# Compressed scores of the prompt with the keys stationary, and three of four groups' normalisation and turning inside the attention loop

## The chip, the cores and the metric

The kernel runs on one core of one Trainium2 chip. Its metric is the time of one execution in device microseconds (us). The engines of the core are TensorE (PE; PEld is its weight load), VectorE (DVE), ScalarE (ACT), GpSimd (POOL) and SyncE (SP). Each takes its own instructions in the order in which they are written; they meet only in semaphores.

## What is computed

One inference step of a hybrid decoder layer: 512 prompt tokens and 8 single decode tokens go through one input projection, an attention group of 16 heads in three branches (compressed, selected, window), a state-space group, an output projection and an MLP. The change lies in the compressed branch of the prompt. There the keys are 31 compressed blocks for each of 4 KV groups, and each group serves 4 heads:

```python
def compressed_attention(q, kc, qpos):
    n_cmp = kc.shape[1]
    s = jnp.einsum('btgrd,bngd->bgrtn', q, kc[:, :, 0]) * ATTN_SCALE
    blk_last = jnp.arange(n_cmp) * CMP_STRIDE + (CMP_BLOCK - 1)
    p = masked_softmax(s, blk_last[None, :] <= qpos[:, None])
    o = jnp.einsum('bgrtn,bngd->btgrd', p, kc[:, :, 1])
    return o.astype(q.dtype), p

def gate_branches(gates, o_cmp, o_sel, o_win):
    return gates[..., 0, None] * o_cmp + gates[..., 1, None] * o_sel + gates[..., 2, None] * o_win
```

For 512 tokens the selected branch covers all blocks, so the two other branches are causal attention of 512 queries over 512 keys, with keys and values of their own.

## The kernel before

The program is one long list for each engine, without a scheduler: the order of the functions at its end (L2421 onward) and the order of the lines in them is the order of the work. The stages around the change, with their lines, are these.

- The input projection ends with `proj`, the projected columns of all 520 tokens, transposed. `rows_*` (L735 to L772) turns keys and values back into token order and writes them out.
- `stack_act` and `stack_dve` (L916 to L950) make the operands of the prompt's attention. PE multiplies in a short float format (fp32r), so a query head of 64 rows is stacked over its own rounding rest in one tile of 128 rows: ACT writes the high part (L923, 64x512), DVE the rest (L940). The keys of a branch and group get two tiles, high over high (`k_hh`) and rest over rest (`k_ll`): ACT writes one half of `k_hh` (L930), DVE both halves of `k_ll` (L949, two instructions) and the second half of `k_hh` (L950). The list `STACKED` holds 16 steps: 4 steps with 8 query heads, 4 with keys (groups 0 and 1, both branches), then the same for the other 8 heads and groups 2 and 3. A key tile lies where a projected query column lay; so the table `K_AFTER` makes a key step wait for query steps (`as_lo`).
- `gate_act` (L978 to L981) puts the gates through a sigmoid. `cmp_p_*` (L805 to L850) makes the compressed keys and values: first layer on PE (L813), sum on DVE (L842), SiLU on ACT (L834), second layer on PE (L818, L823), bias on DVE (L847, L850). `kcp_high` and `kcp_low` (L956, L966, L967) split the keys into `kc_hh` and `kc_ll`, 32 columns for each group. `q_dve` (L1416) puts the decode tokens' queries in place.
- `att_cmp_pe/dve/act` (L985 to L1071) is the compressed attention of the prompt. `scores_c(g)` takes, for each of 4 heads and 4 tiles of 128 queries, the queries as weights and streams 32 columns of `kc_hh` and of `kc_ll`: 32 matmuls a group, in bank 4 or 5 of PSUM by turns (`CB`). DVE adds the mask, takes the maximum and subtracts it (`shifted`, L1025 to L1032), ACT takes the exponential (L1064), DVE sums, inverts, multiplies by the gate and scales (`normed`, L1038 to L1048), PE turns the result with 4 transposes into bank 6 (L1012), and ACT copies it to `kv_tok` (L1070), where the values' product later reads it (`pcT`). Groups 2 and 3 take the banks and buffers of groups 0 and 1. All four groups are through before the attention loop turns its first probabilities.
- `att_pe/dve/act` (L1085 to L1195) is the attention loop: 32 units `u`, one for each head (`h = u // 2`) and branch (`b`). In a unit PE does the scores of unit u+1 (`score`, L1081 to L1083, 4 query tiles into banks 0 to 3), the value product of unit u-1 (`values`, L1112, and at odd units the compressed branch, L1117) and ten transposes of the probabilities of unit u (`turn`, L1100, banks 4 to 6). DVE does `factors` (L1162 to L1168), the maxima of unit u+1 (`row_max`, L1156), the finished head at even units (`head_out`, L1174) and two copies of turned probabilities (`turned`, L1182, L1184). ACT does the exponentials of unit u+1 (`exps`, L1138) and one copy (L1148). Unit 0's `score` stands ahead of the loop, in `att_cmp_pe`.

On POOL, `q_pool` (L1263) clears `qz` and `values_pool` (L802) then clears `vbd`. After the loop come the decode tokens' attention, the state-space part, the output projection and the MLP; none of them is touched.

## Time and profile before

| | us |
|---|---|
| median of 3 runs | 2975.57 |
| their range | 2968.17 to 2980.98 |
| profiled execution | 2988.49 |
| its span in the trace | 2986.8 |

| stretch of the trace, us | what runs |
|---|---|
| 704 to 717 | turning of keys and values |
| 717 to 750 | stacking, gates, compressed keys and values |
| 750 to 796 | compressed attention of the prompt, and `score` of unit 0 |
| 796 to 974 | attention loop |

The page of the profile gives the busy time of each engine over the span; the timelines give single instructions with their start, and in brackets how long the engine had been idle and what released it. A row with a count merges instructions of one kind that follow one another. The duration of a matmul holds the time of its way through the array, so the pace of matmuls is read from start to start. PEclk is the granted clock of TensorE, 1.00 for 2.4 GHz and 0.50 for 1.2 GHz.

### The profile page before, as it was taken

How to read it: one execution, taken by the hardware profiler on the slowest of the kernel's cores; microseconds unless marked ns; L12 is line 12 of the kernel's file. 1: busy time of each engine (PE TensorE's matmuls, PEld its weight loads, DVE VectorE, ACT ScalarE, POOL GpSimd, SP SyncE). 2: the span in 40 equal slices, each digit the busy share in tenths (PEclk: the TensorE clock that was granted, in tenths of full speed). 3: DMA queues.
4: the chain of work that ended last, by engine and by line, in shares of the span. 5: the costliest groups of instructions: out<-in, count | busy, mean ns of one | idle time of the engine just before them, and what ended most of it. 6: DMA issues, size and time to landing. Idle time of an engine off the chain costs nothing.

```text
span 2986.8 us, 51003 instructions
## 1 busy us (share of the span) xinstructions
PE 2820.8 (94%) x21260; PEld 2613.5 (88%) x21260; DVE 1122.8 (38%) x1659; ACT 803.9 (27%) x1277; POOL 103.9 (3%) x115
## 2 busy tenths in 40 slices
PE   4899999996899978989999999999999999999998
PEld 4449999996788635689899999999999999999998
DVE  2322222225588266454333233333333333333333
ACT  1213111114254123443222221222212222122233
POOL 0000000000000002201100000000000000000001
PEclk9999999998699988799999999999999999999999
DMA  5135333332001852322222222222222222222222
GB/s 185 71 114 169 92 91 91 91 86 79 2 1 43 263 204 79 96 95 93 85 86 91 92 91 91 92 91 91 91 91 91 91 91 91 91 91 91 92 91 85
DMA packets 251881, 287.16 MB, mean 96 GB/s; under 512 B 21549, under 2 KB 244139, under 8 KB 247814
## 3 DMA queue, kind: packets, MB, share of 16 engines
q1 hardware_dynamic: 249214, 239.99, 25.7%
q0 software_dynamic: 2592, 46.14, 4.0%
q8 instruction: 51, 0.84, 0.1%
q14 instruction: 24, 0.20, 0.0%
HBM read 273.68 MB, written 20.71 MB: 99 GB/s over the span
## 4 chain that ended last, share of the span: by engine, by line
PE 90%; DVE 4%; DMA 3%; ACT 2%; issue 1%; SPq 0%; POOL 0%; ACTq 0%; POOLq 0%; DVEq 0%
PE PS L610 70%; PE PS L382 4%; PE PS L1112 2%; PE PS L1100 1%; DMA win_t<-kvs_tok 1%; PE PS L1081 1%; PE PS L1878 1%; DMA sel_t<-in_cache_kv_sel,idx_s 1%; PE PS L1365 1%; PE PS L368 1%; PE PS L1832 1%; PE PS L1082 1%; DMA seg_raw<-in_cache_kv_cmp,idx_c 1%; PE PS L1329 1%; DVE seg_ord L464 1%
## 5 line engine op out<-in xcount | busy, mean ns | idle before, releaser
L597 DVE TENSOR_TENSOR w_lo<-w_raw,w_hi 128x1024 fp32r<-128x1024 f32 (+1 forms) x388 | 460.3, 1190 | 1378.6 <-ACT w_hi L591 1377.6
L591 ACT ACTIVATE w_hi<-w_raw 128x1024 fp32r<-128x1024 f32 (+1 forms) x388 | 395.6, 1024 | 1502.1 <-PE PS L610 1502.0
L610 PE MATMUL PS<-h_hi,w_hi 128*128 128x260 f32 x3360 | 675.3, 282 | 7.4 <-DVE w_lo L597 5.1
L610 PE MATMUL PS<-h_lo,w_hi 128*128 128x260 f32 x3360 | 675.2, 282 | 0.0
L610 PE MATMUL PS<-h_hi,w_lo 128*128 128x260 f32 x3360 | 673.9, 282 | 0.0
L610 PEld LDWEIGHTS PS<-h_hi,w_hi 128*128 128x128 f32 x3360 | 516.4, 189 | 8.2 <-issue 7.5
L610 PEld LDWEIGHTS PS<-h_lo,w_hi 128*128 128x128 f32 x3360 | 519.2, 189 | 0.0
L610 PEld LDWEIGHTS PS<-h_hi,w_lo 128*128 128x128 f32 x3360 | 518.1, 189 | 0.0
L610 PE MATMUL PS<-u_hi,w_hi 128*128 128x260 f32 x2048 | 411.3, 282 | 8.4 <-DVE u_lo L2279 8.4
L610 PE MATMUL PS<-u_lo,w_hi 128*128 128x260 f32 x2048 | 410.6, 282 | 0.0
L610 PE MATMUL PS<-u_hi,w_lo 128*128 128x260 f32 x2048 | 410.0, 281 | 0.0
L610 PEld LDWEIGHTS PS<-u_hi,w_hi 128*128 128x128 f32 x2048 | 313.7, 188 | 10.1 <-issue 10.1
L610 PEld LDWEIGHTS PS<-u_lo,w_hi 128*128 128x128 f32 x2048 | 315.5, 188 | 0.0
L610 PEld LDWEIGHTS PS<-u_hi,w_lo 128*128 128x128 f32 x2048 | 314.8, 188 | 0.0
L382 PE MATMUL PS<-segT,w 128*128 128x512 f32 x256 | 110.8, 593 | 0.0
L610 PE MATMUL PS<-mix_hi,w_hi 128*128 128x260 f32 x512 | 103.6, 284 | 7.5 <-DVE w_lo L597 7.5
L610 PE MATMUL PS<-mix_lo,w_hi 128*128 128x260 f32 x512 | 103.5, 284 | 0.0
L610 PE MATMUL PS<-mix_hi,w_lo 128*128 128x260 f32 x512 | 103.2, 283 | 0.0
L382 PEld LDWEIGHTS PS<-segT,w 128*128 128x128 f32 x256 | 48.3, 190 | 59.5 <-issue 59.3
L2169 DVE TENSOR_TENSOR x_acc<-PS,x_acc 128x520 f32 (+1 forms) x144 | 93.5, 691 | 11.2 <-PE PS L610 11.2
L1138 ACT ACTIVATE prob<-PS,negmax 128x128 f32<-128x128 f32 (+3 forms) x128 | 65.8, 526 | 79.1 <-DVE negmax L1156 79.1
L610 PEld LDWEIGHTS PS<-mix_hi,w_hi 128*128 128x128 f32 x512 | 79.3, 190 | 7.6 <-issue 7.6
(394 smaller groups left out, 2463.0 us busy)
## 6 DMA issues: line engine op xcount, KB each, us to landing
w_raw<-in_w_up SPq DMA_DIRECT2D x256, 256.0 KB, 2.8
w_raw<-in_w_down SPq DMA_DIRECT2D x256, 256.0 KB, 2.8
w_raw<-in_w_in SPq DMA_DIRECT2D x160, 256.0 KB, 2.9
w_raw<-in_w_out SPq DMA_DIRECT2D x64, 256.0 KB, 3.0
out_kv_win_s<-in_state_kv_win SPq DMA_DIRECT2D x8, 1022.0 KB, 7.7
win_t<-in_state_kv_win SPq DMA_DIRECT2D x16, 448.0 KB
xtok<-in_x_prompt SPq DMA_DIRECT2D x4, 1024.0 KB, 9.1
x_r<-in_x_prompt SPq DMA_DIRECT2D x4, 1024.0 KB, 6.3
```

Source lines behind the costliest of these rows:

```text
L368: last = e.transpose(PS[:, f % 4, x * P:x * P + P], seg_ord[:, cg, j:j + 2, :].rearrange("p j d -> p (j d)"), ident[:])
L382: last = e.matmul(PS[:, 4 + 2 * c + r, :], w1[:, c, r, j, :], segT[:, t % 2, 4 * c:4 * c + 4, j, :], start=(j == 0), stop=(j == 7))
L464: e.tensor_copy(seg_ord[:, cg], seg_raw[:, :, cg, :]).then_inc(c_order, 1)
L591: ins = e.activation(hi, raw, ACT.Copy)
L597: ins = e.tensor_tensor(lo, raw, hi.bitcast(F32), ALU.subtract)
L610: mm = e.matmul(PS[:, bank + 2 * m + h, 0:HN], w, x[:, k0 + k, h * HN:h * HN + HN], start=st and c == 0, stop=sp and c == 2)
L1081: e.matmul(PS[:, qt, 0:w], q, k_hh[b][g][:, 0:w], start=True, stop=False)
L1082: e.matmul(PS[:, qt, 0:w], q, k_ll[b][g][:, 0:w], start=False, stop=False)
L1100: last = e.transpose(PS[:, 4 + n, c0 + (qt - kt) * P:c0 + (qt - kt) * P + P], prob[:, u % 2, c:c + P], ident[:])
L1112: last = e.matmul(PS[:, 7, kt * P:SEQ], kv_tok[:, kt, c:c + P], probT(u, kt), start=(b == 0 and kt == 0), stop=False)
L1138: e.activation(prob[:, u % 2, P_OFF[qt]:P_OFF[qt] + w], PS[:, qt, 0:w], ACT.Exp, bias=negmax[:, u % 2, qt:qt + 1], accum_out=den[:, u % 2, ...
L2169: e.tensor_tensor(x_acc[:, tile], PS[:, bank:bank + 2, 0:HN], x_acc[:, tile], ALU.add).then_inc(g_out, 1)
```

## The change

Five things are changed.

1. **Compressed scores.** The keys become the weights and the queries are streamed. `kc_pad` holds, for high part and rest and each group, 224 columns, zero but for 32 in the middle. A window of 128 columns that is moved by 32 for each head of the group puts that head's scores into its own 32 rows of the result; 8 matmuls of 512 columns, accumulated in bank `g`, take the place of 32 matmuls of 32 columns. The result lies with keys in the rows; ACT copies it to `sc_T` (`scores_out`), and PE turns it back with 4 transposes into the same bank (`back`). DVE's first step reads it in another order (tile, head, key).
2. **A bank and buffer per group.** `pc`, `pc_e` and `sc_T` exist four times, scores lie in banks 0 to 3. `shifted` runs for all four groups in a row, and only group 0 is normalised ahead of the loop. `score` of unit 0 stands behind `ac_sub` 4, since it writes banks 0 to 3.
3. **Inside the loop.** DVE normalises groups 1 to 3 at the end of units 3, 11 and 19 (`PC_NORM`). PE turns groups 0 to 3 in units 0, 6, 14 and 22 (`PC_TURN`), between `score` and `values`, and ACT copies them there between `exps` and its own copy. The last two transposes of `turn` in these units wait for that copy, since they write bank 6 too.
4. **Stacking in two halves.** `stack_*` does steps 0 to 7, then gates and compressed keys come, and then steps 8 to 15; on ACT these stand behind `scores_out` of groups 0 and 1.
5. **Second half of `k_hh`** is written by a second ACT instruction and no longer by DVE. POOL clears `kc_pad` once the first layer's products are done, and `kcp_high` waits for it.

```diff
-        kc_hh = at("kc_hh", [P, NKV, 32], SB + 2880, F32R)
-        kc_ll = at("kc_ll", [P, NKV, 32], SB + 3392, F32R)
+        kc_pad = at("kc_pad", [P, 2, NKV, 224], A0 + 16384, F32R)
+        kc_hh, kc_ll = (kc_pad[:, x, :, 96:128] for x in range(2))
         prob = at("prob", [P, 2, 1280], A0 + 16640)
         vbd = at("vbd", [P, 2, 4, P], A0 + 26880)
         pt_x = at("pt_x", [P, 512], A0 + 30976)
-        pc = [at(f"pc{x}", [P, 16, 32], A0 + 2048 * x) for x in range(2)]
-        pc_e = [at(f"pc_e{x}", [P, 16, 32], A0 + 4096 + 2048 * x) for x in range(2)]
+        pc = [at(f"pc{x}", [P, 16, 32], A0 + 2048 * x) for x in range(NKV)]
+        pc_e = [at(f"pc_e{x}", [P, 16, 32], A0 + 8192 + 2048 * x) for x in range(NKV)]
+        sc_T = [at(f"sc_T{x}", [P, SEQ], A0 + 8192 + 2048 * x) for x in range(NKV)]
         P_OFF = [P * qt * (qt + 1) // 2 for qt in range(4)]
...
-        def stack_act(e):
+        def stack_act(e, first, end):
             e.wait_ge(g_out, NTILE)
             e.wait_ge(q_kept, 1)
-            for n, (kind, x, y) in enumerate(STACKED):
+            for n in range(first, end):
+                kind, x, y = STACKED[n]
...
-                    e.activation(k_hh[x][y][rows_, :], pt[rows_, K_TILE[x] + y // 2, 0:SEQ],
-                                 ACT.Copy).then_inc(as_hi, 2)
-
-        def stack_dve(e):
-            for n, (kind, x, y) in enumerate(STACKED):
+                    for to in (rows_, slice((1 - a) * HD, (1 - a) * HD + HD)):
+                        e.activation(k_hh[x][y][to, :], pt[rows_, K_TILE[x] + y // 2, 0:SEQ],
+                                     ACT.Copy).then_inc(as_hi, 1)
+
+        def stack_dve(e, first, end):
+            for n in range(first, end):
+                kind, x, y = STACKED[n]
...
-                        e.tensor_tensor(k_ll[x][y][to, :], src, hh[rows_, :].bitcast(F32), ALU.subtract)
-                    e.tensor_copy(hh[other, :], hh[rows_, :].bitcast(F32)).then_inc(as_lo, 2)
+                        e.tensor_tensor(k_ll[x][y][to, :], src, hh[rows_, :].bitcast(F32),
+                                        ALU.subtract).then_inc(as_lo, 1)
 
         def kcp_high(e):
             e.wait_ge(*p_out(2))
+            e.wait_ge(n_free, 2)
             for a in range(2):
...
-        CB = (4, 5)
-
         def att_cmp_pe(e):
 
+            def scores_c(g):
+                e.wait_ge(as_lo, 8 if g < 2 else 24)
+                for r in range(4):
+                    for x in range(2):
+                        last = e.matmul(PS[:, g, :], kc_pad[:, x, g, 96 - 32 * r:224 - 32 * r],
+                                        q_st[:, 4 * g + r, :], start=(r + x == 0), stop=(r + x == 4))
+                last.then_inc(ac_s, 1)
+
+            def back(g):
+                e.wait_ge(ac_out, g + 1)
+                for qt in range(4):
+                    last = e.transpose(PS[:, g, qt * P:qt * P + P], sc_T[g][:, qt * P:qt * P + P], ident[:])
+                last.then_inc(ac_back, 1)
+
             e.wait_ge(kc_lo, 2)
+            e.wait_ge(*p_out(3))
+            e.wait_ge(*a_gate(2))
+            for g in (0, 2):
+                scores_c(g)
+                scores_c(g + 1)
+                back(g)
+                back(g + 1)
             e.wait_ge(as_lo, 2 * len(STACKED))
-
-            def scores_c(g):
...
-                        e.matmul(PS[:, CB[g % 2], c:c + 32], w, kc_hh[:, g, :], start=True, stop=False)
-                        last = e.matmul(PS[:, CB[g % 2], c:c + 32], w, kc_ll[:, g, :], start=False, stop=True)
-                last.then_inc(ac_s, 1)
-
-            scores_c(0)
-            scores_c(1)
             e.wait_ge(*a_mask(2))
-            e.wait_ge(*a_gate(2))
+            e.wait_ge(ac_sub, NKV)
             for qt in range(4):
                 score(e, 0, qt)
-            for g in range(NKV):
-                e.wait_ge(ac_p, g + 1)
-                if g:
-                    e.wait_ge(ac_Tc, g)
...
+        PC_TURN = {max(0, 8 * g - 2): g for g in range(NKV)}
+        PC_NORM = {8 * g - 5: g for g in range(1, NKV)}
+
+        def pc_turn(e, u, g):
+            e.wait_ge(ac_p, g + 1)
+            if u:
+                e.wait_ge(as_td, 2 * u)
+            for r in range(4):
+                last = e.transpose(PS[:, 6, r * P:r * P + P],
+                                   pc_e[g][:, 4 * r:4 * r + 4, :].rearrange("p t n -> p (t n)"), ident[:])
+            last.then_inc(ac_T, 1)
+
+        def pc_copy(e, g):
+            e.wait_ge(ac_T, g + 1)
+            h = 4 * g
+            for half in range(2):
+                pair = kv_tok[:, h % 8 // 2 + half, KVW * (1 + h // 8):KVW * (1 + h // 8) + 2 * P]
+                last = e.activation(pair, PS[:, 6, half * 256:half * 256 + 256], ACT.Copy)
+            last.then_inc(ac_Tc, 1)
+
+        def pc_normed(e, ch, g):
...
-                p, mx = pc[g % 2], cmx[:, g % 2]
-                e.wait_ge(ac_s, g + 1)
...
+                p, mx = pc[g], cmx[:, g % 2]
+                e.wait_ge(ac_back, g + 1)
+                ch.step(e.tensor_tensor(p[:].rearrange("p (r t) n -> p t r n", r=4),
+                                        PS[:, g, :].rearrange("p (t r n) -> p t r n", t=4, r=4),
+                                        cmpmask[:].unsqueeze(2).to_broadcast([P, 4, 4, 32]), ALU.add))
                 ch.settle()
                 ch.step(e.tensor_reduce(mx, p[:], AX.X, ALU.max))
                 ch.settle()
                 e.tensor_tensor(p[:], p[:], mx.unsqueeze(2).to_broadcast([P, 16, 32]), ALU.subtract).then_inc(ac_sub, 1)
...
             e.wait_ge(*a_gate(1))
-            shifted(0)
             for g in range(NKV):
-                if g + 1 < NKV:
-                    shifted(g + 1)
-                normed(g)
+                shifted(g)
+            pc_normed(e, ch, 0)
 
         def att_cmp_act(e):
+            def scores_out(g):
+                e.wait_ge(ac_s, g + 1)
+                e.activation(sc_T[g][:], PS[:, g, :], ACT.Copy).then_inc(ac_out, 1)
+            scores_out(0)
+            scores_out(1)
+            stack_act(e, 8, len(STACKED))
+            scores_out(2)
+            scores_out(3)
+            for g in range(NKV):
+                e.wait_ge(ac_sub, g + 1)
+                e.activation(pc_e[g][:], pc[g][:], ACT.Exp).then_inc(ac_exp, 1)
             e.wait_ge(rows_out, 16 * N_ROWS_OUT)
...
         def att_pe(e):
             def turn(u):
                 e.wait_ge(as_sc, u + 1)
-                if u == 0:
-                    e.wait_ge(ac_sub, NKV)
-                    e.wait_ge(ac_Tc, NKV)
                 for n, kts in enumerate(((0,), (1, 3), (2,))):
                     if u and n == 0:
                         e.wait_ge(as_ta, u)
...
+                    if n == 2 and u in PC_TURN:
+                        e.wait_ge(ac_Tc, PC_TURN[u] + 1)
...
                 if b:
                     e.wait_ge(v_bd, 16 * 4)
+                    e.wait_ge(ac_Tc, h // 4 + 1)
                     for qt in range(4):
                         last = e.matmul(PS[:, 7, qt * P:qt * P + P], vbd[:, h // 8, qt, :], pcT(h),
                                         start=False, stop=(qt == 3))
...
                 if u + 1 < NU:
                     for qt in range(4):
                         score(e, u + 1, qt)
+                if u in PC_TURN:
+                    pc_turn(e, u, PC_TURN[u])
                 if u:
                     values(u - 1)
                 turn(u)
...
             for u in range(NU):
                 if u + 1 < NU:
                     exps(u + 1)
+                if u in PC_TURN:
+                    pc_copy(e, PC_TURN[u])
                 e.wait_ge(as_T, 3 * u + 1)
                 if u >= 2:
                     e.wait_ge(as_pv, u - 1)
...
                 if u and u % 2 == 0:
                     head_out(u // 2 - 1)
                 turned(u)
+                if u in PC_NORM:
+                    pc_normed(e, ch, PC_NORM[u])
             head_out(NH - 1)
 
         PV_ORDER = (6, 7, 0, 1, 2, 3, 4, 5)
...
+            e.wait_ge(*p_prod(4))
+            e.memset(kc_pad[:].bitcast(F32), 0.0).then_inc(n_free, 1)
 
         def smp_pool(e, ch):
             e.wait_ge(as_s, 4 * NU)
...
-            stack_act(e)
+            stack_act(e, 0, 8)
             gate_act(e)
             cmp_p_act(e)
...
-            stack_dve(e)
+            stack_dve(e, 0, 8)
             cmp_p_dve(e)
+            stack_dve(e, 8, len(STACKED))
             q_dve(e, ch)
```

On ACT, from the stacking to the compressed attention, the kernel before has this order (`proj` the projected columns, `sc_T` the copied scores, `pc` and `pc_e` the shifted scores and their exponentials):

```order
L923 ACTIVATE q_st<-proj 64x512 x8
L930 ACTIVATE k_hh_113<-proj 64x512
L930 ACTIVATE k_hh_114<-proj 64x512
L930 ACTIVATE k_hh_117<-proj 64x512
L930 ACTIVATE k_hh_118<-proj 64x512
L978 ACT_TABLE_LOAD
```

and the changed kernel, from the split of the compressed keys on:

```order
L961 ACTIVATE kc_pad<-kcp_T 64x2x32 x2
L1077 ACTIVATE sc_T_152<-PS 128x512
L1077 ACTIVATE sc_T_153<-PS 128x512
L925 ACTIVATE q_st<-proj 64x512 x8
L933 ACTIVATE k_hh_113<-proj 64x512 x2
L933 ACTIVATE k_hh_114<-proj 64x512 x2
L933 ACTIVATE k_hh_117<-proj 64x512 x2
L933 ACTIVATE k_hh_118<-proj 64x512 x2
L1077 ACTIVATE sc_T_154<-PS 128x512
L1077 ACTIVATE sc_T_155<-PS 128x512
```

The second half of the stacking has moved from ahead of the gates to behind the copies of the first two groups' scores. On DVE, between the compressed keys and the first maxima, the kernel before has (`cmx` the maxima):

```order
L966 TENSOR_TENSOR kc_ll<-kcp_T,kc_hh 64x2x32 x2
L967 CAST kc_hh<-kc_hh 64x2x32
L1416 COPY qz<-q_smp 64x8 x16
L1025 TENSOR_TENSOR pc_145<-PS,cmpmask 128x512
L1030 TENSOR_REDUCE cmx<-pc_145 128x16
```

and the changed kernel:

```order
L972 CAST kc_pad<-kc_pad 64x2x32
L944 SCALAR_TENSOR_TENSOR q_st<-proj,q_st 64x512 x8
L953 TENSOR_TENSOR k_ll_121<-proj,k_hh_113 64x512 x2
L953 TENSOR_TENSOR k_ll_122<-proj,k_hh_114 64x512 x2
L953 TENSOR_TENSOR k_ll_125<-proj,k_hh_117 64x512 x2
L953 TENSOR_TENSOR k_ll_126<-proj,k_hh_118 64x512 x2
L1439 COPY qz<-q_smp 64x8 x16
L1061 TENSOR_TENSOR pc_144<-PS,cmpmask 128x4x4x32
L1065 TENSOR_REDUCE cmx<-pc_144 128x16
L1067 TENSOR_TENSOR pc_144<-pc_144,cmx 128x512
```

The second half of the stacking has come between the split of the compressed keys and the copies to `qz`. On PE the changed kernel has, between the second layer and unit 0's scores:

```order
L823 MATMUL PS<-w_95,hidp_s 31x64 x4
L994 MATMUL PS<-q_st,kc_pad 128x512 x16
L1001 MATMUL PS<-ident,sc_T_152 128x128 x4
L1001 MATMUL PS<-ident,sc_T_153 128x128 x4
L994 MATMUL PS<-q_st,kc_pad 128x512 x16
L1001 MATMUL PS<-ident,sc_T_154 128x128 x4
L1001 MATMUL PS<-ident,sc_T_155 128x128 x4
L1096 MATMUL PS<-k_hh_111,q_st 128x128
```

The 128 matmuls with queries as weights (L997, L998) are gone from here, and so are three of the four groups' transposes, which now lie in the loop.

## Rows read from the trace of the kernel before

**Rows 1.** The page, part 1: busy time, share and instructions of each engine.

```profile
PE 2820.8 (94%) x21260; PEld 2613.5 (88%) x21260; DVE 1122.8 (38%) x1659; ACT 803.9 (27%) x1277; POOL 103.9 (3%) x115
```

**Rows 2.** Busy time by stretch; columns start:end, length, engines, PEclk, DMA share, GB/s.

```profile
726.00:746.00 20.00, 0.07 (x1) 0.00 (x0) 17.80 (x31) 11.08 (x21) 0.00 (x0) 0.62 0.00 0
746.00:796.00 50.00, 36.48 (x172) 34.67 (x172) 21.08 (x61) 7.75 (x18) 0.00 (x0) 0.50 0.01 3
796.00:806.00 10.00, 9.40 (x41) 8.06 (x42) 7.12 (x22) 5.94 (x23) 0.00 (x0) 0.68 0.01 2
812.00:850.00 38.00, 38.00 (x242) 31.82 (x241) 31.71 (x88) 18.45 (x63) 0.00 (x0) 1.00 0.00 1
```

**Rows 3.** Timeline of ACT: start, us, line, op, operands, count, [idle before <-releaser].

```profile
717.00 5.20 ACT L923 ACTIVATE q_st<-proj 64x512 fp32r<-64x512 f32 x8
723.45 2.59 ACT L930 ACTIVATE k_hh<-proj 64x512 fp32r<-64x512 f32 x4 [1.26 <-issue]
...
742.44 1.28 ACT L978 ACT_TABLE_LOAD   x1
...
795.54 0.66 ACT L1070 ACTIVATE kv_tok<-PS 128x256 f32<-128x256 f32 x2 [1.44 <-PE PS L1012]
...
802.26 0.59 ACT L1148 ACTIVATE kv_tok<-PS 128x512 f32<-128x512 f32 x1
```

**Rows 4.** Timeline of DVE, the same columns.

```profile
717.66 5.71 DVE L940 SCALAR_TENSOR_TENSOR q_st<-proj,q_st 64x512 fp32r<-64x512 f32 x8 [1.74 <-ACT q_st L923]
724.12 1.38 DVE L949 TENSOR_TENSOR k_ll<-proj,k_hh 64x512 fp32r<-64x512 f32 x2 [0.75 <-ACT k_hh L930]
...
745.32 0.48 DVE L842 TENSOR_TENSOR hid_p<-PS,second_p 128x124 f32<-128x124 f32 x2
...
749.96 1.60 DVE L1416 COPY qz<-q_smp 64x8 f32<-64x8 f32 x16
...
763.85 0.69 DVE L1025 TENSOR_TENSOR pc<-PS,cmpmask 128x512 f32<-128x512 f32 x1 [4.62 <-PE PS L998]
...
765.91 0.68 DVE L1038 TENSOR_REDUCE cden<-pc_e 128x16 f32<-128x512 f32 x1
...
798.27 0.18 DVE L1162 RECIPROCAL rec<-den 128x4 f32<-128x4 f32 x1 [2.34 <-ACT prob L1138]
```

**Rows 5.** Timeline of POOL, the same columns.

```profile
717.09 1.80 POOL L1263 MEMSET qz<- 128x2048 f32 x1 [605.89 <-ACT segp_T L746]
```

**Rows 6.** Timeline of PE, the same columns.

```profile
746.78 0.64 PE L818 MATMUL PS<-hidp_s,w 128*64 128x31 f32 x8 [20.71 <-ACT hidp_s L834]
...
749.98 0.39 PE L997 MATMUL PS<-kc_hh,q_st 128*128 128x32 f32 x1 [1.57 <-DVE kc_hh L967]
...
763.65 0.45 PE L1081 MATMUL PS<-k_hh,q_st 128*128 128x128 f32 x1
...
765.82 0.73 PE L1081 MATMUL PS<-k_hh,q_st 128*128 128x512 f32 x1
766.36 0.63 PE L1082 MATMUL PS<-k_ll,q_st 128*128 128x512 f32 x1
766.78 0.31 PE L1083 MATMUL PS<-cm_r,id_r 128*128 128x128 f32 x1
768.13 1.11 PE L1012 MATMUL PS<-ident,pc_e 128*128 128x128 f32 x4 [1.04 <-DVE pc_e L1048]
...
792.29 1.11 PE L1012 MATMUL PS<-ident,pc_e 128*128 128x128 f32 x4 [4.33 <-DVE pc_e L1048]
...
800.01 2.40 PE L1100 MATMUL PS<-ident,prob 128*128 128x128 f32 x10
802.06 0.46 PE L1081 MATMUL PS<-k_hh,q_st 128*128 128x128 f32 x1
```

**Rows 7.** Timeline of DVE and of PE inside the attention loop, unit 4.

```profile
824.64 0.41 DVE L1184 COPY kv_tok<-PS 128x256 f32<-128x256 f32 x1
...
825.68 2.37 PE L1112 MATMUL PS<-kv_tok 128*128 128x512 f32 x8
```

More of the change, by code:

```diff
@@ L889, in build_program @@
         kc_hi, kc_lo = sem("kc_hi"), sem("kc_lo")
-        ac_s, ac_sub, ac_exp, ac_p, ac_T, ac_Tc = (
-            sem(n) for n in ("ac_s", "ac_sub", "ac_exp", "ac_p", "ac_T", "ac_Tc"))
+        ac_s, ac_out, ac_back, ac_sub, ac_exp, ac_p, ac_T, ac_Tc = (
+            sem(n) for n in ("ac_s", "ac_out", "ac_back", "ac_sub", "ac_exp", "ac_p", "ac_T", "ac_Tc"))
         as_s, as_max, as_exp, as_fac, as_sc, as_T, as_ta, as_td, as_pv, as_o = (
@@ new lines, in pc_normed @@
+        def pc_normed(e, ch, g):
+            gv = gates[:].rearrange("p t (h b) -> p h t b", b=3)
+            p, dn, rc, fc = pc_e[g], cden[:, g % 2], crec[:, g % 2], cfac[:, g % 2]
+            e.wait_ge(ac_exp, g + 1)
+            ch.step(e.tensor_reduce(dn, p[:], AX.X, ALU.add))
+            ch.settle()
+            ch.step(e.reciprocal(rc, dn))
+            ch.settle()
+            ch.step(e.tensor_tensor(fc.rearrange("p (r t) -> p r t", t=4), rc.rearrange("p (r t) -> p r t", t=4),
+                                    gv[:, 4 * g:4 * g + 4, :, 0], ALU.mult))
+            ch.settle()
+            ch.step(e.tensor_scalar(cfac[:, g % 2, 0:16:4], cfac[:, g % 2, 0:16:4], valid0[:, 0:1], None, ALU.mult))
+            ch.settle()
+            e.tensor_tensor(p[:], p[:], fc.unsqueeze(2).to_broadcast([P, 16, 32]), ALU.mult).then_inc(ac_p, 1)
```

43 lines of the change are left out of this document (removed).

## The prediction, made before the changed kernel was run

> **What bounds the kernel now.** I read the page first, then the busy time by stretch, then the timelines of the four engines where PE stands still. Over the whole span PE is busy 94% of the time [rows 1], so a gain has to come either out of PE's work or out of one of the few places where PE waits. The stretches show such a place [rows 2]: from 726 to 746 PE does nothing while DVE is busy 17.8 of 20 us, and from 746 to 796 PE is busy 36.5 of 50 us, but at a granted clock of 0.50, which is 1.2 GHz. From 802 on it is full again, and inside the attention loop PE is busy all the time at 1.00, with DVE busy 31.7 of 38 us and ACT 18.5. So from 726 to about 802 DVE's and PE's chains set the pace by turns, and in the loop PE does. The timelines name the links. PE waits 20.71 us for the SiLU of the compressed keys' first layer and gets it at 746.78 [rows 6], because its sum on DVE comes only at 745.32 [rows 4], behind the whole stacking, and ACT's sigmoid table only at 742.44 [rows 3]. Then two groups' scores take PE from 749.98 to 763.65 [rows 6]: 64 matmuls of 32 columns at 0.21 us each, although they stream little. The groups' softmax on DVE and their transposes follow, the third of them at 792.29, and the first `turn` runs from 800.01 to 802.06 [rows 6]. This end, 802.06, is my landmark: behind it PE is the bound, so what comes earlier there comes earlier at the end.
>
> **Compressed keys ahead of the second half of the stacking.** Eight query parts take ACT 5.20 and DVE 5.71 us [rows 3, 4], as before. The four key steps then cost ACT two instructions each, 8 x 0.65 from 723.45 = 728.65; DVE loses its copy, starts when the first pair is there (724.8) and takes 4 x 1.39, to 730.3. The table load of 742.44 thus comes at 728.65, 13.8 us earlier, and the chain from there to the SiLU hangs on ACT: the same steps that led from 742.44 to PE's start at 746.78. DVE is free at 730.3 for the sum, which is wanted at 731.1. So second layer, bias and split all move by 13.8 us: PE's L818 from 746.78 to 733.0, the first score from 749.98 to 736.2 [rows 6]. The clearing of `kc_pad` is 1792 elements a row, nearest to `qz` with 2048 in 1.80 us [rows 5]; it runs from 726.1 on POOL and is wanted at 734.1, so it costs nothing, and up to 6 us of delay would still be hidden. The clearing of `vbd` behind it is wanted only by the value copies after 734.
>
> **Scores of groups 0 and 1.** 16 matmuls of 512 columns with a weight load each. No row has just this; the nearest are the two 512-wide ones of `score` at the same clock, 0.54 and 0.42 us from start to start [rows 6]. The mean of 0.48 gives 7.7 us, to 743.9; at full clock it would be half, to 740.1. PE has by then stood still since 726 but for the second layer, so it starts at 0.50; before, by the mean of 0.68 over 796 to 806 [rows 2], it came back at about 802.4, some 6 us after PE's last wait, which would be 742 here. I take 743.2 with the array's way out, and 0.60 for ACT's copy of group 1 (its L1148 copy of the same shape takes 0.59 [rows 3]): 743.8. On this the Trainium skill ("TensorE: Matmul & The Clock Gate", "Back-to-back issue gap") gives 512 columns 426.7 ns cold, which hides the weight load wholly; the rows agree for one of the two matmuls and not for the other. By the page the end would be 0.6 us earlier.
>
> **Second half of the stacking.** ACT comes to it at 743.8, since `scores_out` stands ahead, so DVE stands still from 736.1 to 744.5. This is what the order costs: 8.4 us. Then DVE's 5.71 us for the queries, to 750.2. ACT may write the keys of steps 12 and 13 after that (751.5), DVE subtracts (4 x 0.69, to 754.3), ACT does steps 14 and 15 (755.7), DVE ends at 758.5. The copies to `qz`, 1.60 [rows 4], to 760.1. Beside this PE does groups 2 and 3 from 750.2 to 757.9 and turns them back by 759.6, ACT's last copy ends at 758.7. Only groups 0 and 1 are wanted by DVE at 760.1, so this is hidden with about 5 us to spare for group 2.
>
> **Shift, first normalisation, unit 0.** `shifted` takes 2.06 a group (763.85 to 765.91 [rows 4]); four in a row 8.3, to 768.4. I take the other reading order at no extra cost, as the count of elements is the same; if the first of its three steps took twice its 0.69, this would be 2.8 longer. Normalising group 0 takes 2.1 (PE's transposes at 768.13 follow on 765.91 [rows 4, 6]), to 770.5. `score` of unit 0 starts at 768.4 and takes 3.44 at 0.50 (from 763.65 to the idle time of 1.04 ahead of 768.13 [rows 6]), to 771.9; this is now late and is the new wait of this place. The last maximum is there at 772.7, the last exponential at 773.5. `factors` begins at 773.6 instead of 798.27 [rows 4], so `turn` of unit 0 may start at 775.2. PE reaches it at 775.5, behind `score` of unit 1 and 0.9 us of turning group 0. ACT is through with the exponentials of unit 1 at 777.6, as far behind `factors` as 802.26 was behind 798.27 [rows 3, 4], then copies group 0 in 0.66 [rows 3], to 778.2, and only then may the last two transposes go: 778.6 at 0.2 each. The landmark moves from 802.06 to 778.6, **23.5 us** earlier.
>
> **In the loop.** Three times four transposes at full clock, half of 0.205 each (ten take 2.05 at 0.50 [rows 6]): 12 x 0.10 = 1.2 us of PE work that is put back, on the path. Their ACT copies, 3 x 0.66, have ACT's idle half beside them; I take 0. The three normalisations put 2.1 us each into DVE's queue at the end of an odd unit, ahead of `factors`, and behind these stand the maxima and so the exponentials and the next scores. DVE idles 6.3 us in 38 [rows 2], about 0.9 a unit. In unit 4 its last copy ends at 825.05 and PE's `values` that waits for it starts at 825.68 [rows 7], 0.6 to spare. So 2.1 - 0.9 - 0.6 leaves 0.6 of waiting at most places; part of it is taken up by DVE's own waits elsewhere, and I take 0.4 each, 1.2 in all, with 0 and 2.1 each as the ends.
>
> **Sum.** -23.5 + 1.2 + 1.2 = **-21.1 us**. Against the profiled execution's 2988.5 that is 2967.4. The median of the runs shown is 2975.57, 12.9 below the profiled execution; the difference carries over, so the time is 2975.6 - 21.1 = **2954.5**, or -0.7%. What a measurement of this kernel can tell from no change is about 0.5%, 14.9 us.
>
> **The rivals.**
>
> A, the loop gives it back: DVE is busy 83% in the loop, and a normalisation stalls PE by its whole 2.1 us and for a unit more. Three times 2.1, with 2.8 for a slower first step in `shifted`, leaves 23.5 - 1.2 - 6.3 - 2.8 = 13.2, or 2962; with one of the two, some 16 to 18, or 2958 to 2960. For it: DVE is the engine with the least air beside PE. Against: the 0.6 and 0.9 above.
>
> B, the clock comes back sooner: PE's new work at 736 and 768 is of long matmuls, and if the clock rises within the head, `score` of units 0 and 1, the back turns and the first `turn` take half. `score` 1.7 less, the scores of group 1 up to 2 less, the end of `turn` 0.5: gain 25, or 2950.
>
> C, slower than before: the head no longer gives PE 50 us of work ahead of the loop, only bursts with 6 and 9 us of idling between them, and the loop could start and stay at 0.50. A pair of units takes 10.8 at 1.00 (802 to 974 in the table of stretches, 16 pairs), so each pair at 0.50 costs 10.8 more. The gain is gone after two pairs, and from 3.3 pairs on (36 us) the kernel is over 0.5% slower: with four pairs 2954.5 + 43 = 2998. Against it: before, PE had stood idle 4.33 us just ahead of 792.29 [rows 6], at 0.50 all along, and the stretch 796 to 806 has a mean of 0.68 [rows 2], so it was back at 1.00 at about 802.4.
>
> D, it does not do what it says: the head is bound by DVE's sum of work and this is not less, only the 64 matmuls of groups 2 and 3 go. DVE's idle 8.4 us would then be larger, by what PE needs more for its 16 matmuls with `kc_pad`: if a window of weights that starts inside a padded tile took twice a usual matmul, 7.7 more in the first two groups, gain 13, or 2962. Nothing in the rows speaks for it.
>
> **How the numbers follow.** The forecast, a gain of 18 to 24, has 0.60. A has 0.17, B 0.11, D 0.08, C 0.04. The runs of the same kernel lie 7 below and 5 above their median, which I add in part. Low end: B with 4 more, 2946; high end: A and D with 5 more, 2967. C stays out. Faster by over 0.5% is the forecast, B and half of A and D, less the runs' scatter: 0.79. Within 0.5%: 0.17. Slower: 0.04.
>
> **What would show it.** In the changed trace the SiLU should start near 732.5 and the first 512-wide score near 736.2, at 0.4 to 0.55 us a matmul; DVE should idle some 8 us just before its second set of `q_st` subtractions near 744.5; its four shifts should end near 768.4 and unit 0's score follow at once; the first `turn` should end near 778.6. In the loop units 3, 11 and 19 should each be followed by a PE wait of under 1 us for DVE's copy, and units 6, 14 and 22 be longer by 0.4. I am wrong if the loop's units at 1.00 have grown elsewhere, if the clock rows of 780 to 960 show 0.50, or if a stretch behind 960 is longer than before.

## The result and the profile after

The changed kernel takes 2965.9 us (median of 20 runs, 2951.3 to 2979.0), the kernel before 2983.0 (20 runs, 2968.2 to 2994.9): a ratio of 0.994, with a 95% interval of 0.9924 to 0.9956. By the ratio that is 18 us, with 13 to 23. A second set of 12 runs gives 0.9954 (0.9937 to 0.9972). The forecast was 2954.5 us, which is 21.1 under the median of 2975.6 of three runs, with a range of 2946 to 2967. The measured time lies in it, 1.1 us from its upper end and 11.4 above the forecast: 7.4 of these because the three runs lay that much below the median of twenty, and some 3 to 4 because the gain was smaller.

The first lines of the page, with the columns of [rows 1]:

```profile
span 2977.1 us, 50867 instructions
...
PE 2820.4 (95%) x21180; PEld 2605.2 (88%) x21180; DVE 1120.0 (38%) x1651; ACT 810.3 (27%) x1289; POOL 105.4 (4%) x116
```

The profiled span is 9.7 us shorter, less than the medians say. To read where the time went I cut each trace at four instructions that all kernels have: PE's first product of the compressed keys' first layer (L813), unit 2's first score (the landmark of the prediction), the decode tokens' first matmul, and the output projection's first. The stretches between are called the head, the loop and the decode and state-space part. Busy time of the three, columns as in [rows 2], of the kernel before:

```profile
717.03:802.06 85.03, 50.98 (x258) 48.53 (x259) 49.45 (x114) 30.41 (x64) 2.76 (x2) 0.56 0.08 28
802.06:973.65 171.59, 169.52 (x1056) 141.04 (x1055) 138.04 (x385) 82.14 (x274) 1.97 (x2) 1.00 0.07 26
973.65:1292.44 318.79, 275.87 (x1261) 173.50 (x1260) 158.99 (x275) 105.28 (x249) 46.13 (x40) 0.82 0.48 154
```

and of the changed kernel:

```profile
720.37:781.03 60.66, 32.76 (x166) 27.61 (x167) 41.28 (x91) 36.27 (x72) 4.29 (x3) 0.75 0.11 39
781.03:957.41 176.38, 173.83 (x1069) 143.47 (x1068) 143.37 (x399) 82.83 (x278) 1.97 (x2) 0.99 0.06 25
957.41:1281.09 323.68, 285.31 (x1262) 179.52 (x1260) 158.94 (x275) 105.09 (x249) 46.09 (x40) 0.80 0.47 152
```

The head is 24.4 us shorter (85.0 to 60.7), the loop 4.8 longer (171.6 to 176.4), in sum 19.6. The rest of what the two spans tell is elsewhere, where nothing was edited: the changed kernel's trace reaches the head 3.3 us later, the third stretch is 4.9 longer, and what lies behind it 1.7. The third stretch's mean granted clock is 0.80, and 0.82 before. The 3.3 us and the third stretch are taken up below.

The head of the changed kernel on PE, which answers to [rows 6]. The head starts at 720.37 here and at 717.03 before, so 3.3 is to be taken off a time to compare it with the prediction:

```profile
736.29 0.64 PE L818 MATMUL PS<-hidp_s,w 128*64 128x31 f32 x8 [6.89 <-ACT hidp_s L834]
...
739.49 6.16 PE L994 MATMUL PS<-q_st,kc_pad 128*128 128x512 f32 x16 [1.57 <-DVE kc_pad L972]
...
752.72 6.35 PE L994 MATMUL PS<-q_st,kc_pad 128*128 128x512 f32 x16 [5.74 <-DVE q_st L944]
760.01 1.14 PE L1001 MATMUL PS<-ident,sc_T 128*128 128x128 f32 x8 [0.94 <-ACT sc_T L1077]
771.14 0.45 PE L1096 MATMUL PS<-k_hh,q_st 128*128 128x128 f32 x1 [9.99 <-DVE pc L1067]
...
776.80 0.60 PE L1027 MATMUL PS<-ident,pc_e 128*128 128x128 f32 x4
777.89 1.09 PE L1114 MATMUL PS<-ident,prob 128*128 128x128 f32 x8 [0.48 <-DVE prob L1187]
780.84 0.44 PE L1114 MATMUL PS<-ident,prob 128*128 128x128 f32 x2 [1.86 <-ACT kv_tok L1036]
781.03 0.30 PE L1096 MATMUL PS<-k_hh,q_st 128*128 128x128 f32 x1
```

on DVE, which answers to [rows 4]:

```profile
746.96 5.70 DVE L944 SCALAR_TENSOR_TENSOR q_st<-proj,q_st 64x512 fp32r<-64x512 f32 x8 [7.53 <-ACT q_st L925]
754.01 2.84 DVE L953 TENSOR_TENSOR k_ll<-proj,k_hh 64x512 fp32r<-64x512 f32 x4 [1.35 <-ACT k_hh L933]
...
762.71 0.69 DVE L1061 TENSOR_TENSOR pc<-PS,cmpmask 128x512 f32<-128x512 f32 x1
...
770.91 0.68 DVE L1043 TENSOR_REDUCE cden<-pc_e 128x16 f32<-128x512 f32 x1
...
776.14 0.18 DVE L1181 RECIPROCAL rec<-den 128x4 f32<-128x4 f32 x1 [0.84 <-ACT prob L1155]
```

and on ACT, which answers to [rows 3]:

```profile
731.96 1.28 ACT L983 ACT_TABLE_LOAD   x1
...
745.68 0.60 ACT L1077 ACTIVATE sc_T<-PS 128x512 f32<-128x512 f32 x1 [1.78 <-PE PS L994]
746.30 5.20 ACT L925 ACTIVATE q_st<-proj 64x512 fp32r<-64x512 f32 x8
...
780.14 0.65 ACT L1036 ACTIVATE kv_tok<-PS 128x256 f32<-128x256 f32 x2
```

The second layer starts 15.9 us after the first product (29.8 before). Sixteen 512-wide matmuls take 6.0 us (739.49 to the transposes that follow at 745.48). PE later waits 5.74 for DVE's query parts, and 9.99 for its last shift. DVE's first run of queries of the second half starts at 746.96, 7.5 us after it was free, since ACT's copies begin only at 746.30, behind the score copy of 745.68. The first `turn` waits 1.86 for ACT's copy of 780.14, as foretold.

### The profile page after: what moved, and what is told of

It is laid out like the page before. It is cut to its first block, busy times and chain, and to the rows that moved or that the text cites. A ratio compares the mean times of both kernels' runs of the same rounds, so it can differ in the third digit from the quotient of the medians.

```text
span 2977.1 us, 50867 instructions
## 1 busy us (share of the span) xinstructions
PE 2820.4 (95%) x21180; PEld 2605.2 (88%) x21180; DVE 1120.0 (38%) x1651; ACT 810.3 (27%) x1289; POOL 105.4 (4%) x116
## 4 chain that ended last, share of the span: by engine, by line
PE 89%; DVE 4%; DMA 3%; ACT 2%; issue 1%; SPq 0%; POOL 0%; ACTq 0%; POOLq 0%; DVEq 0%
PE PS L610 70%; PE PS L382 4%; PE PS L1126 2%; DMA sel_t<-in_cache_kv_sel,idx_s 1%; PE PS L1114 1%; PE PS L1096 1%; PE PS L1901 1%; PE PS L368 1%; DMA win_t<-kvs_tok 1%; PE PS L1855 1%; PE PS L1097 1%; PE PS L1918 1%; DMA seg_raw<-in_cache_kv_cmp,idx_c 1%; PE PS L1388 1%; DVE seg_ord L464 1%
## 5 line engine op out<-in xcount | busy, mean ns | idle before, releaser
L610 PEld LDWEIGHTS PS<-u_lo,w_hi 128*128 128x128 f32 x2048 | 315.6, 189 | 0.0
L610 PEld LDWEIGHTS PS<-u_hi,w_lo 128*128 128x128 f32 x2048 | 314.9, 188 | 0.0
```

The costliest lines, as they stand in the source:

```text
L610: mm = e.matmul(PS[:, bank + 2 * m + h, 0:HN], w, x[:, k0 + k, h * HN:h * HN + HN], start=st and c == 0, stop=sp and c == 2)
```

## Experiments

All numbers of head and loop are from one trace each. They repeat: a second trace of the kernel before gave 85.07 and 171.65, of the changed kernel 60.70 and 176.33, so differences of 0.3 us can be read there, while the whole runs of either kernel lie some 27 us apart from the lowest to the highest. The times of e4 and e6 rest on 4 runs each, those of e5 and e8 on 6 and 7, the others on 10 or more.

| kernel | head | loop | both | decode and state-space (its mean clock) | time against before |
|---|---|---|---|---|---|
| before | 85.0 | 171.6 | 256.6 | 318.8 (0.82) | 1 |
| changed | 60.7 | 176.4 | 237.0 | 323.7 (0.80) | 0.994 (0.9924 to 0.9956) |
| c_after | 60.7 | 176.3 | 237.0 | 312.8 (0.84) | 0.9954 (0.9937 to 0.9972) |
| e1_norm_head | 66.6 | 172.6 | 239.2 | 325.2 (0.80) | 0.9971 (0.9953 to 0.999) |
| e2_split_only | 74.2 | 171.8 | 246.1 | 319.2 (0.82) | 0.9966 (0.9944 to 0.9987) |
| e3_act_order | 54.2 | 176.3 | 230.5 | 314.0 (0.81) | 0.9936 (0.991 to 0.9962) |
| e4_queries_weights | 58.8 | 174.7 | 233.6 | 319.4 (0.83) | 0.9905 (0.987 to 0.9939) |
| e6_norm_parts | 60.7 | 174.2 | 234.9 | 302.9 (0.85) | 0.9904 (0.9875 to 0.9932) |
| e7_turn_unit1 | 58.6 | 176.1 | 234.7 | 315.6 (0.83) | 0.9934 (0.991 to 0.9957) |
| e5_all | 50.7 | 175.0 | 225.6 | 315.0 (0.81) | 0.9914 (0.9888 to 0.994) |
| e8_all_again | 50.5 | 174.9 | 225.3 | 314.9 (0.81) | 0.9906 (0.987 to 0.9943) |

### One part alone: the stacking in two halves

```diff
-            stack_act(e)
+            stack_act(e, 0, 8)
             gate_act(e)
             cmp_p_act(e)
+            stack_act(e, 8, len(STACKED))
             att_cmp_act(e)
```

On DVE the second half stands between `cmp_p_dve` and `q_dve`, and the wait of `scores_c` on `as_lo` is 16 for groups 0 and 1.

> The kernel before with one part of the change alone: the stacking in two halves, steps 8 to 15 behind the compressed keys on ACT and DVE. Scores, banks, buffers, and all four groups' normalisation and turning as in the kernel before. Theory (half of the head's gain is this part: the compressed keys come 14 us sooner, and the second half of the stacking hides under the first two groups' scores on PE): the second layer on PE 15.7 after the first product and not 29.8; head 85.0 - 10 = 75; loop 171.6. Rival (DVE's sum of work is the same and sets the head, so little comes of it): head 82 or more.

The head is 74.2, 10.8 shorter than before. Timeline of PE in this kernel, waits only:

```profile
732.00 0.64 PE L818 MATMUL PS<-hidp_s,w 128*64 128x31 f32 x8 [5.85 <-ACT hidp_s L834]
...
735.20 0.40 PE L999 MATMUL PS<-kc_hh,q_st 128*128 128x32 f32 x1 [1.57 <-DVE kc_hh L969]
...
769.51 1.11 PE L1014 MATMUL PS<-ident,pc_e 128*128 128x128 f32 x4 [4.33 <-DVE pc_e L1050]
...
781.59 1.11 PE L1014 MATMUL PS<-ident,pc_e 128*128 128x128 f32 x4 [4.33 <-DVE pc_e L1050]
```

The second layer starts 14.9 us after the first product (732.00, from 717.11), and what follows is the old chain: a group's 32 matmuls, its shift and its normalisation, with 4.33 us of waiting for DVE twice. So this part alone brings 10.8 of the 24.4 us, and the rest of the change on top of it 13.6.

### One part undone: queries as weights again

```diff
-                    for x in range(2):
-                        last = e.matmul(PS[:, g, :], kc_pad[:, x, g, 96 - 32 * r:224 - 32 * r],
-                                        q_st[:, 4 * g + r, :], start=(r + x == 0), stop=(r + x == 4))
+                    for qt in range(4):
...
+                        e.matmul(PS[:, g, c:c + 32], w, kc_hh[:, g, :], start=True, stop=False)
+                        last = e.matmul(PS[:, g, c:c + 32], w, kc_ll[:, g, :], start=False, stop=True)
```

`kc_hh` and `kc_ll` are the slices of `kc_pad` that hold the keys. `back` and `scores_out` are no longer called, and `shifted` waits for `ac_s` and reads the scores in the order of before. Banks, buffers, the halves of the stacking and the work in the loop stay as in the changed kernel.

> The queries are the weights again, 32 matmuls of 32 columns a group, straight into banks 0 to 3, with no copy by ACT and no turning back; banks, buffers, stacking in halves and the work inside the loop as in the changed kernel. Theory (the order of ACT's queue costs what the longer matmuls save): PE needs 4 x 6.8 us at 0.50 from the keys on and is done 27.4 us after, DVE's last shift 2.1 behind; head 58.7, up to 60.5 if the clock stays at 0.50 through units 0 and 1. Rival (keys as weights is what brings the gain): head 68 or more.

The head is 58.8, 1.9 shorter than in the changed kernel, and the loop 1.6 shorter. PE and then DVE, timelines:

```profile
737.85 0.40 PE L996 MATMUL PS<-kc_pad,q_st 128*128 128x32 f32 x1 [1.57 <-DVE kc_pad L972]
...
767.66 0.45 PE L1093 MATMUL PS<-k_hh,q_st 128*128 128x128 f32 x1 [2.32 <-DVE pc L1068]
```

```profile
765.37 0.69 DVE L1061 TENSOR_TENSOR pc<-PS,cmpmask 128x512 f32<-128x512 f32 x1 [4.69 <-PE PS L997]
```

PE works without a break from 737.85 on, 27.4 us for four groups, more than twice what the 512-wide matmuls need. Still DVE has its last scores at 765.37, since ACT goes on with the stacking at once. So with the keys as weights, which give the change its name, head and loop are 3.5 us longer as they are placed: 1.9 in the head, and 1.6 in the loop, where this kernel's clock did not fall (below). In the head it is the place of `scores_out` on ACT, not the form of the matmuls, that costs this: in the next kernel the head with the keys as weights is 4.6 shorter than this one. The 1.6 of the loop are there in the next kernel too. The gain is of the other parts: 10.5 us in head and loop come with the halves of the stacking alone (e2), and the 12.5 between e2 and this kernel with the remaining parts: a bank and buffer for each group, the work moved into the loop, and the second half of `k_hh` on ACT. Of these only the place of the normalisations was run by itself (below).

### The order on ACT

```diff
+            stack_act(e, 8, 12)
             scores_out(0)
             scores_out(1)
-            stack_act(e, 8, len(STACKED))
+            stack_act(e, 12, len(STACKED))
```

> The eight query copies of the second half of the stacking go ahead of the copies of the first two groups' scores on ACT; all else as in the changed kernel. Theory (DVE's 7.5 us of waiting before these queries lie on the path that sets the head): head 60.7 - 6.4 = 54.3, the key steps then wait for the second score copy; loop unchanged. Rival (PE's scores or ACT bind at once in its place): head within 1 us of 60.7.

The head is 54.2, 6.5 shorter. DVE's timeline:

```profile
737.93 5.71 DVE L944 SCALAR_TENSOR_TENSOR q_st<-proj,q_st 64x512 fp32r<-64x512 f32 x8
746.00 2.84 DVE L953 TENSOR_TENSOR k_ll<-proj,k_hh 64x512 fp32r<-64x512 f32 x4 [2.36 <-ACT k_hh L933]
```

The queries start at 737.93, at once behind the compressed keys, and the keys then wait 2.36 us, partly for the second score copy. Of 7.5 us of DVE's waiting, 6.5 were on the path.

### Where the normalisations stand

```diff
-        PC_NORM = {8 * g - 5: g for g in range(1, NKV)}
+        PC_NORM = {}
...
+            for g in range(NKV):
+                pc_normed(e, ch, g)
```

> Groups 1 to 3 are normalised ahead of the loop, right behind group 0, and not in units 3, 11 and 19; all else as in the changed kernel. Theory (in the loop each normalisation costs PE 0.7 us of its 2.1, ahead of the loop it is all on DVE's path): head 60.7 + 5.6 = 66.3, loop shorter by 2.1, in sum 3.5 longer. Rival A (a normalisation in the loop costs its whole 2.1): the sum stays or falls by 0.7.

The head is 66.6, 5.9 longer; the loop is 3.75 shorter and not 2.1, so the sum of both is 2.1 longer and not 3.5. What is left over the loop of before is 1.0, about the 12 transposes. Of the 3.75, 1.6 are not of the normalisations: the next kernel keeps them in the loop at no cost and its loop is 1.6 longer than this one's. In this kernel the clock does not fall in the loop, and in the next and in the changed one it does.

> Each normalisation in the loop is cut in three parts in successive units: the sum (0.7 us) at the end of unit 2, 10 and 18, the inverse and the factors (0.7) one unit later, the scaling (0.7) one more. All else as in the changed kernel. Theory (DVE has about 1.3 us to spare a unit, so 2.1 at once costs 0.7 and 0.7 at a time nothing): head 60.7, loop 176.3 - 2.1 = 174.2. Rival (the cost comes from the work, not from its being in one piece): loop within 0.5 of 176.3.

The edit: `PC_NORM = {8 * g - 6 + x: (g, x) for g in range(1, NKV) for x in range(3)}`, with `pc_normed` cut in three. The head is the same, the loop 174.2, 2.1 shorter, as expected. So three normalisations in one piece cost 0.7 each, and in three pieces nothing. Units 3 to 6 of the changed kernel on PE:

```profile
797.48 1.26 PE L1114 MATMUL PS<-ident,prob 128*128 128x128 f32 x10
...
803.39 1.31 PE L1114 MATMUL PS<-ident,prob 128*128 128x128 f32 x10
...
806.79 2.39 PE L1126 MATMUL PS<-kv_tok 128*128 128x512 f32 x8 [0.17 <-issue]
809.02 1.26 PE L1114 MATMUL PS<-ident,prob 128*128 128x128 f32 x10
...
811.80 0.60 PE L1027 MATMUL PS<-ident,pc_e 128*128 128x128 f32 x4
...
815.29 1.25 PE L1114 MATMUL PS<-ident,prob 128*128 128x128 f32 x10
```

From `turn` to `turn` the units take 5.91, 5.63 and 6.27 us; before, the same three took 5.87, 4.99 and 5.87. The unit behind the normalisation is 0.64 longer, of which 0.17 shows as a wait. The rest lies in matmuls that start later one after another: from this unit's first score to its value product 2.34 us pass (804.45 to 806.79), and 1.74 in e6, where the normalisation is in parts. The unit with the group's transposes is 0.40 longer.

### The clock inside the loop

Stretches of the changed kernel around the first turn:

```profile
777.00:781.80 4.80, 2.46 (x21) 1.99 (x19) 3.51 (x10) 3.21 (x11) 0.00 (x0) 1.00 0.00 0
781.80:785.20 3.40, 3.40 (x10) 2.38 (x9) 3.05 (x10) 1.55 (x7) 0.00 (x0) 0.50 0.00 0
785.20:790.00 4.80, 4.80 (x31) 4.03 (x30) 2.24 (x8) 1.19 (x3) 0.00 (x0) 1.00 0.00 0
```

For 3.4 us at the start of the loop the granted clock is at 0.50. The same stands in the traces of c_after, e3 and e6, each time 0.5 to 1.0 us after the end of a wait of PE in the turn, of 1.86 us (1.85 in c_after and e6). At half the clock 3.4 us lose 1.7, the loops of e1 and e6 are 1.6 apart, and the loop of 176.4 leaves 1.5 for it, over 171.6 with 1.2 for the transposes and 2.1 for the normalisations. The kernel with the queries as weights speaks against the wait as the only cause: it waits 1.86 at the same place, until 777.36, and its clock stays at 1.00. (The expectation of e7, below, says "in every trace with this wait"; that is wrong by this one.) There PE had worked without a break from 737.85 to 765, at 0.50 until 773.2; in the changed kernel it had stood still for 9.99 us ahead of 771.14, and the clock was back at 775.0.

```diff
-        PC_TURN = {max(0, 8 * g - 2): g for g in range(NKV)}
+        PC_TURN = {max(1, 8 * g - 2): g for g in range(NKV)}
```

> Group 0 is turned and copied in unit 1 and not in unit 0; all else as in the changed kernel, in which PE waits 1.9 us in unit 0's turn for ACT's copy of group 0, and the granted clock then falls to 0.50 for 3.4 us within the loop, in every trace with this wait. Theory (the fall follows from PE's standing still in the turn, and costs 1.5 us): head 60.7 - 2.1 = 58.6; no fall in the loop; loop 176.3 - 1.5 + 0.4 = 175.2. Rival (the fall is by the long wait ahead of unit 0, which stays): loop 176.7.

Timeline of PE, waits and turns of units 0 and 1:

```profile
777.90 1.31 PE L1114 MATMUL PS<-ident,prob 128*128 128x128 f32 x10 [0.93 <-DVE prob L1187]
...
783.53 1.04 PE L1114 MATMUL PS<-ident,prob 128*128 128x128 f32 x8
785.13 0.41 PE L1114 MATMUL PS<-ident,prob 128*128 128x128 f32 x2 [0.56 <-ACT kv_tok L1036]
```

Group 0's copy is no longer waited for in unit 0, the head is 58.6, and the clock does not fall in the loop. The loop is 176.1 all the same, 0.9 more than expected: the stretch from unit 2's first score to unit 3's takes 6.33, against 4.96 in the kernel with the queries as weights, which has neither the transposes nor a fall there. Read from start to start, the four transposes take 0.45 of this (780.93 to 781.38), the last two transposes of the turn start 0.8 later than usual, of which 0.56 shows as the wait, and the rest lies in the scores ahead of them. So the copy is still waited for, and the gain of the clock is spent on it. In sum 2.3 us are won. Without the wait in unit 0 there was no fall, in one kernel, and with it there was one in four of five.

That a wait of this size does not decide by itself is shown by a part that no edit touches, far ahead of the head. Twice in each trace PE waits 2.41 us for DVE and then does 44 transposes of `seg_ord`. The first place of the kernel before, of the changed kernel and of the combined kernel e5, and of its repetition e8:

```profile
104.67 5.02 PE L368 MATMUL PS<-ident,seg_ord 128*128 128x128 f32 x44 [2.41 <-DVE segT L456]
104.69 6.69 PE L368 MATMUL PS<-ident,seg_ord 128*128 128x128 f32 x44 [2.41 <-DVE segT L456]
103.48 6.69 PE L368 MATMUL PS<-ident,seg_ord 128*128 128x128 f32 x44 [2.41 <-DVE segT L456]
104.13 5.02 PE L368 MATMUL PS<-ident,seg_ord 128*128 128x128 f32 x44 [2.41 <-DVE segT L456]
```

Where they take 6.69, the granted clock is at 0.50 for 3.4 us (106.0 to 109.4 in the changed kernel). Of the 24 such places in twelve traces 14 have such a fall within 1.4 us of the wait's end. The program of e5 and e8 has it at the first place in one trace and at the second in the other. So the same wait in the same program is followed by a fall or not from one execution to the next; what decides stays open, and e7's single trace does not prove that its fall is gone because the wait is.

These falls are also the 3.3 us by which the changed kernel reaches the head later: it has both of them, twice 1.67, in its trace and in its repetition, and the kernel before has none in either of two. Over all runs the three traces without the new scores and buffers (before twice, e2) have none, and the nine others one or two. Whether the change brings them about, by ways that no experiment touched, or this is chance, is not shown; if it does, 16.3 of the 19.6 us are left at the end of the loop.

### The same kernels again

> The changed kernel once more, unedited. Two stretches of the trace are measured in every run: the head, from PE's first product of the compressed keys' first layer (L813) to unit 2's first score, and the loop, from there to the decode tokens' first matmul. Before they were 85.0 and 171.6 us, in the changed kernel 60.7 and 176.4. Theory (the change's work sets both): head 60.7 again within 0.5, loop 174.9 to 176.5, by whether the granted clock dips in it. What comes behind the loop lost about 11 us against before in the one trace of the changed kernel. Theory: that is the scatter of the granted clock in the state-space part and will come out otherwise here, by 3 us or more. Rival (the change hurts what comes behind): the same 11 us again. Time: 0.6% below before, as measured.

> The kernel before once more, unedited, for its stretch from the decode tokens' first matmul to the output projection: 318.8 us in the trace of before, 323.7 and 312.8 in two of the changed kernel. Theory (its length scatters by the granted clock): another value between 312 and 326. Rival (it is 318.8 by the order of the work): within 1 of 318.8. Head 85.0 and loop 171.6 again.

Head and loop come out within 0.1 us. The third stretch of the changed kernel is 312.8 and not 323.7:

```profile
957.43:1270.22 312.79, 271.81 (x1261) 169.91 (x1260) 159.02 (x275) 105.00 (x249) 47.17 (x40) 0.84 0.49 157
```

The same program had a granted clock of 0.84 in it here and of 0.80 there, and 10.9 us less. So this stretch alone scatters by more than half of the measured gain, and the first trace's 4.9 us over the kernel before are no fixed cost of the change. The repeated trace of before, though, gave 318.9 against 318.8, which is what the rival said: two equal values do not show scatter, and what makes one run's clock in this stretch differ from another's stays open. Over all twelve traces the stretch lies between 302.9 (clock 0.85) and 325.2 (0.80); in between the two go together only loosely, as 0.81 goes with 314.0 and 0.82 with 318.8. The two traces of the combined kernel agree as well (315.0 and 314.9), those of the changed kernel alone do not.

### What the runs point to, together

```diff
-            e.wait_ge(ac_sub, NKV)
             for qt in range(4):
+                e.wait_ge(ac_sub, qt + 1)
                 score(e, 0, qt)
...
             row_max(0)
+            pc_normed(e, ch, 0)
```

with ACT's order of e3, the normalisations in parts of e6, the turn in unit 1 of e7, and `q_dve` ahead of DVE's wait for the second layer.

> All that the first runs point to, together, on the changed kernel: ACT's query copies ahead of the score copies; the 16 copies to qz in the gap in which DVE waits for the second layer; the score of unit 0 waits for each bank by itself and not for all four; group 0 is normalised behind the first maxima and turned in unit 1; the three other normalisations in parts. Theory: head 54.2 - 1.6 - 2.2 and about 0.5 for the turn, some 50; loop 173 to 174.6, by whether the clock dips in it; in sum 13 us under the changed kernel's 237.0. Rival (PE or ACT bind sooner): head 53 or more.

> The kernel of e5_all once more, unedited, for its time with more runs: head and loop 225.6 in sum, 31 us less than in the kernel before and 11.4 less than in the changed kernel. Theory (what the head and loop gain reaches the end): time 1.0% below before, 0.990 to 0.9925. Rival (the later parts give it back): 0.994 or more.

The head is 50.7 and 50.5, and head and loop together are 31 us shorter than before and 11.4 and 11.7 shorter than in the changed kernel. PE's waits ahead of the loop:

```profile
751.21 1.14 PE L1002 MATMUL PS<-ident,sc_T 128*128 128x128 f32 x8 [2.92 <-ACT sc_T L1080]
754.56 0.44 PE L1100 MATMUL PS<-k_hh,q_st 128*128 128x128 f32 x1 [2.21 <-DVE pc L1071]
...
760.62 0.80 PE L1100 MATMUL PS<-k_hh,q_st 128*128 128x512 f32 x1 [0.93 <-DVE pc L1071]
...
766.42 2.40 PE L1118 MATMUL PS<-ident,prob 128*128 128x128 f32 x10 [1.28 <-DVE prob L1191]
```

The scores of unit 0 now follow DVE's shifts bank by bank. The loop came out at 175.0 where 173 to 174.6 was expected, for a cost of its own:

```profile
752.00:773.00 21.00, 14.35 (x55) 12.45 (x53) 19.15 (x44) 9.90 (x29) 0.00 (x0) 0.51 0.01 2
773.00:790.00 17.00, 17.00 (x103) 13.75 (x102) 12.63 (x38) 7.01 (x23) 0.00 (x0) 1.00 0.01 1
```

PE works in bursts here, 14.35 of 21 us, and the clock stays at 0.50 until some 4 us into the loop, which begins at 768.47; at half the clock these lose some 2 us. The time is 0.9914 and 0.9906 of before. That beats the kernel before. The intervals of these two overlap with that of the changed kernel, and whole runs do not order the experiments among themselves: e4 and e6 come out as low with 8 to 9.6 us more in head and loop. It is these stretches alone that show the combined kernel ahead.

## Why the prediction was right, point by point

- **Compressed keys 13.8 us sooner.** The first score stood 32.95 us after the first product before and stands at 19.12 now: 13.8.
- **512-wide matmuls.** 7.7 us were taken for 16, 0.48 each at 0.50; it was 6.0, at a mean clock of 0.60, which fits 0.45 at 0.50 and half of that at 1.00. The row of 0.42 was the nearer one. The clock came back within the 16, as taken, 1 us earlier than taken.
- **The order on ACT costs 8.4 us.** DVE waited 7.5, and e3 gave 6.5 of it back. What the section did not price is the sum of this part against its alternative. It names the order as a cost and the small matmuls as PE's work, but never sets the two against each other; e4 shows that without it head and loop would have been 3.5 us shorter, and e3 that in another order on ACT its form does gain. Rival D saw that DVE's idle time is where PE's new matmuls would be paid, but by a slow window of weights, which the 0.45 rules out.
- **The four shifts.** 8.3 forecast, 8.2 measured (762.71 to 770.91); the other reading order costs nothing.
- **Landmark.** 23.5 earlier forecast, 24.4 measured. The 0.9 came nearly all from the first sixteen matmuls, which took 6.0 and not the 7.0 of the working, by their pace and by the clock's earlier return: with 3.3 taken off, DVE's second queries start at 743.6 (744.5 forecast), unit 0's score at 767.8 (768.4) and its `factors` at 772.8 (773.6). That the clock was back at 1.00 from 775.0 on, as in rival B, added at most 0.1 behind that, since `turn` then waited for DVE and ACT.
- **Transposes in the loop.** 1.2, as forecast.
- **Normalisations in the loop.** This term was mis-sized: 0.4 each taken, 0.7 measured. The working gave 0.6 and then took a part off for DVE's own waits elsewhere; 0.6 was near, and the part taken off was not there.
- **The fall of the clock in the loop.** Not forecast, 1.5 us, and put at nothing in the sum. Rival C spoke of a loop that stays at 0.50; it was 3.4 us. The wait behind which it stands was in the prediction, which let the turn's last two transposes wait for ACT's copy until 778.6, with no thought of what could follow it; that it is a part of the cause rests on e7's one trace, against e4 and against the places with 2.41 us above, and is not shown.
- **Signs of being wrong.** Two that the prediction named did come: a row between 780 and 960 at 0.50, for 3.4 us, and a stretch behind 960 longer than before (323.7 against 318.8). The first is the 1.5 us above; the second went to 312.8 in the repetition.
- **Sum.** Head and loop: -21.1 forecast, -19.6 measured; the difference is 0.9 won in the head, 0.9 lost to the normalisations and 1.5 to the clock. The whole run gives -18, with 13 to 23, which cannot tell 19.6 from 21.1. That the time fell in the range owes something to luck: the starting median was 7.4 us too low, and what lies outside head and loop, which the prediction took as unchanged, differed by 3.3 us ahead of the head and by 11 us between two traces of one program behind the loop.

## What to carry to other kernels

A stage that waits in turns on several engines is paid by the engine whose queue is in the wrong order, not by the one with the most work: here a copy at the head of ACT's queue undid, in the head, what longer matmuls had saved on PE. When work is moved into a loop bound by another engine, cut it to pieces smaller than the idle time of one turn. For changes of half a per cent, compare stretches between fixed instructions in the traces; head and loop repeat to 0.2 us here, while whole runs lie 27 apart; and look at the stretches that nobody edited as well.

## What the runs showed of the hardware

- The 32-column matmuls with a new load of 128 weight columns keep a pace of 0.214 us at 0.50 (13.67 us for 64), and the 512-wide ones with a new load each 0.45: sixteen times the columns for twice the time.
- A granted clock of 0.50 for 3.4 us came 0.5 to 1.0 us after PE had stood still for 1.86 us in an otherwise busy stretch, in four traces. A fifth trace has the same wait and no fall. After a wait of 2.41 us elsewhere a fall of the same length came at 14 of 24 places, at different ones in two executions of one program; each cost 1.67 us.
- The decode and state-space part of one and the same program took 10.9 us more at a mean granted clock of 0.80 than at 0.84.
